# Projection and gate tiles: high and low activations as one 512-column matmul, second half of the bank added on VectorE

## What is computed

```python
def parallel_mixers(h, w_in, b_gate, ...):
    proj = h @ w_in          # 1024 -> qa ka va qb kb vb fb qc kc vc gates
    ...
    gates = jax.nn.sigmoid(gl.reshape(bsz, seq, N_BRANCHES, D_MODEL) + b_gate)
    merged = (gates[:, :, 0] * (ya @ w_out_a)
              + gates[:, :, 1] * (yb @ w_out_b)
              + gates[:, :, 2] * (yc @ w_out_c))
    return merged @ w_out
...
for l in range(DEPTH):
    ...
    h = rms_norm(x, norm1_g[l]) * (1.0 + sc1) + sh1
    x = x + g1 * parallel_mixers(h, ...)
    h = rms_norm(x, norm2_g[l]) * (1.0 + sc2) + sh2
    x = x + g2 * peer_ffn(h, ...)
```

## Time and profile before

| | |
|---|---|
| median of the runs | 2226.91 us |
| the profiled execution | 2227.43 us |
| its span, first to last instruction | 2225.6 us |
| TensorE (PE) busy | 97% of the span |
| VectorE (DVE) busy | 74% |
| ScalarE (ACT) busy | 55% |
| GpSimd (POOL) busy | 12% |
| mean granted TensorE clock | 0.989 of full speed |
| read from HBM | 425 MB, 191 GB/s |

### The profile page before, as it was taken

The page is one execution under the profiler, slowest core; times in us unless marked ns, Lnnn a source line. Parts: engine busy times, 40 slices in busy tenths (PEclk is TensorE's granted clock), DMA queues, the critical chain, the costliest instruction groups (busy, mean ns, idle before and its releaser), DMA issues.

```text
span 2225.6 us, 45150 instructions
## 1 busy us (share of the span) xinstructions
PE 2164.8 (97%) x14996; PEld 1996.6 (90%) x14996; DVE 1656.9 (74%) x3155; ACT 1217.0 (55%) x2134; POOL 268.7 (12%) x298
## 2 busy tenths in 40 slices
PE   4999999999999999999989999999999999999998
PEld 4889989999999988888878899899999999888887
DVE  6787766889589956777557868588895998567765
ACT  3656555444577654545455565644445776454544
POOL 0210000000157500000002100000001772000000
PEclk7999999999999999999999999999999999999999
DMA  8566655555533357787545666455555334588765
GB/s 321 169 209 216 209 171 169 180 180 178 185 127 114 114 195 255 253 257 229 196 174 171 224 213 214 138 182 183 180 184 174 114 113 135 195 274 256 254 214 162
DMA packets 114452, 427.48 MB, mean 192 GB/s; under 512 B 12704, under 2 KB 12960, under 8 KB 113056
## 3 DMA queue, kind: packets, MB, share of 16 engines
q1 hardware_dynamic: 114336, 426.08, 57.3%
HBM read 424.98 MB, written 1.05 MB: 191 GB/s over the span
## 4 chain that ended last, share of the span: by engine, by line
PE 94%; DVE 2%; issue 1%; DMA 1%; ACT 1%; POOL 0%; SPq 0%; ACTq 0%; DVEq 0%; POOLq 0%
PE pj L1290 18%; PE pj L1291 17%; PE pj L1292 17%; PE wk L1290 10%; PE wk L1292 10%; PE wk L1291 10%; PE wk L1602 5%; DMA arena<-in_front 1%; PE wk L1402 1%; PE wk L1379 1%; PE wk L1341 1%; PE wk L1395 1%; PE wk L1542 0%; PE wk L1315 0%; PE wk L1424 0%
## 5 line engine op out<-in xcount | busy, mean ns | idle before, releaser
L797 DVE TENSOR_TENSOR lo<-raw,hi 128x1024 fp32r<-128x1024 f32 x683 | 840.3, 1232 | 475.8 <-ACT hi L471 468.0
L471 ACT ACTIVATE hi<-raw 128x1024 fp32r<-128x1024 f32 x683 | 721.6, 1057 | 468.6 <-PE wk L1292 345.1
L1290 PE MATMUL pj<-mov_hi,hi 128*128 128x256 f32 x3248 | 945.5, 291 | 31.6 <-DVE mov_lo L848 27.5
L1291 PE MATMUL pj<-mov_lo,hi 128*128 128x256 f32 x3248 | 921.3, 284 | 0.0
L1292 PE MATMUL pj<-mov_hi,lo 128*128 128x256 f32 x3248 | 921.2, 284 | 0.0
L1290 PEld LDWEIGHTS pj<-mov_hi,hi 128*128 128x128 f32 x3248 | 624.2, 192 | 47.1 <-DVE mov_lo L848 30.4
L1291 PEld LDWEIGHTS pj<-mov_lo,hi 128*128 128x128 f32 x3248 | 625.9, 193 | 0.2
L1292 PEld LDWEIGHTS pj<-mov_hi,lo 128*128 128x128 f32 x3248 | 624.9, 192 | 0.0
L1290 PE MATMUL wk<-hi,mov_hi 128*128 128x512 f32 x1024 | 398.6, 389 | 1.7 <-DVE mov_lo L1239 1.7
L1292 PE MATMUL wk<-hi,mov_lo 128*128 128x512 f32 x1024 | 398.4, 389 | 0.0
L1291 PE MATMUL wk<-lo,mov_hi 128*128 128x512 f32 x1024 | 398.4, 389 | 0.0
(11 more groups left out here) (184 smaller groups left out, 1507.9 us busy)
## 6 DMA issues: line engine op xcount, KB each, us to landing
raw<-in_stream SPq DMA_DIRECT2D x684, 512.0 KB, 3.3
arena<-in_ada SPq DMA_DIRECT2D x72, 512.0 KB, 4.8
onehot_a<-in_ada SPq DMA_DIRECT2D x24, 512.0 KB, 4.6
arena<-in_front SPq DMA_DIRECT2D x4, 2048.0 KB, 19.3
arena<-in_taba SPq DMA_DIRECT2D x2, 1536.0 KB, 19.4
arena<-in_keys SPq DMA_DIRECT2D x2, 1024.0 KB, 6.3
x<-in_xT SPq DMA_DIRECT2D x1, 1024.0 KB, 5.0
arena<-in_mix SPq DMA_DIRECT2D x2, 512.0 KB, 16.1
```

What stands on the lines that cost most here:

```text
L471: nc.scalar.activation(hi[j % SPLIT][:, :], raw[j % RAW][:, :], ACT.Copy).then_inc(hi_done, 1)
L797: nc.vector.tensor_tensor(lo[j % SPLIT][:, :], raw[j % RAW][:, :], hi[j % SPLIT][:, :].bitcast(f32), ALU.subtract).then_inc(lo_done, 1)
L1290: pe.matmul(out, w_h, m_h, start=first, stop=False)
L1291: pe.matmul(out, w_h, m_l, start=False, stop=False)
```

## The change

The high and low activations of the 8 chunks are laid side by side in one buffer `mov`, so that 512 columns of one chunk are contiguous. For the 47 tiles of a layer that are neither V tiles nor outside the input projection, a new `project_half` issues two matmuls a chunk in place of three: the high weights by high and low activations at once, over all 512 columns of the bank, and the low weights by the high activations into the first 256. ScalarE evicts the first half as before, but raises a new semaphore `first_half`. VectorE then adds the second half to what was evicted (`second_half_of`), and it raises `out_free`. The new VectorE instruction for tile t-1 is put at the very start of VectorE's step t. All other stages keep three matmuls; they read `mov` through `mov_hi(k)`, `mov_lo(k)` and `mov_of`. The branch outputs and the one-hot buffers that used chunks 8 to 11 of the old buffers have their own `w_hi` and `w_lo`.

```diff
-        mov_hi = sb("mov_hi", [P, 12, SEQ], f32r)
-        mov_lo = sb("mov_lo", [P, 12, SEQ], f32r)
+        mov = sb("mov", [P, KC, 2, SEQ], f32r)
+        w_hi = sb("w_hi", [P, 4, SEQ], f32r)
+        w_lo = sb("w_lo", [P, 4, SEQ], f32r)
...
@@ evict, ScalarE @@
                     if t < N_QKV:
                         nc.scalar.activation(projT[:, t, :], pj[t % 2][:, 0:SEQ], ACT.Identity,
-                                             scale=HD ** -0.5 if QC <= t < QC + 4 else 1.0).then_inc(out_free, 1)
+                                             scale=HD ** -0.5 if QC <= t < QC + 4 else 1.0).then_inc(first_half, 1)
...
@@ VectorE @@
+                def second_half_of(t):
+
+                    if VB <= t < VB + 4 or VC <= t < VC + 4:
+                        return
+                    before = t - 4 * (t > VB) - 4 * (t > VC)
+                    dve.wait_ge(first_half, l * (DENSE - 8) + before + 1)
+                    if t in (VB + 4, VC + 4):
+
+                        dve.wait_ge(out_free, l * OUTS + t + 2)
+                    nc.vector.scalar_tensor_tensor(projT[:, t, :], pj[t % 2][:, SEQ:2 * SEQ],
+                                                   HD ** -0.5 if QC <= t < QC + 4 else 1.0, projT[:, t, :], ALU.mult,
+                                                   ALU.add).then_inc(out_free, 2 if t == DENSE - 1 else 1)
+
                 for t in range(DENSE):
+                    if t:
+                        second_half_of(t - 1)
...
                     if t in ADA_AT:
                         modulation(ADA_AT.index(t))
+                second_half_of(DENSE - 1)
                 rest_of(L0 + (DENSE + AHEAD), DENSE + AHEAD)
...
@@ TensorE @@
+                def project_half(t, j, o, bank, chunks=None, between=None):
+
+                    pe.wait_ge(lo_done, t + 1)
+                    pe.wait_ge(out_free, l * OUTS + o + 1)
+                    out = pj[bank][:, :]
+                    for k in range(KC):
+                        if chunks is not None:
+                            pe.wait_ge(mov_ready, l * M_READY + (chunks + k + 1))
+                        if between is not None and k == KC // 2:
+                            between()
+                        wh, wl = chunk(j, k)
+                        both = mov[:, k, :, :].rearrange("p a s -> p (a s)")
+                        if k < KC - 1:
+                            pe.matmul(out, wh, both, start=k == 0, stop=False)
+                            pe.matmul(out[:, 0:SEQ], wl, mov_hi(k), start=False, stop=False)
+                        else:
+                            pe.matmul(out[:, 0:SEQ], wl, mov_hi(k), start=False, stop=False)
+                            last = pe.matmul(out, wh, both, start=False, stop=True)
+                    return last
...
-                        project(L0 + t, t, t, t % 2, None if t else 0, between=lambda: late_pieces(t))\
+                        project_half(L0 + t, t, t, t % 2, None if t else 0, between=lambda: late_pieces(t))\
```

More of the change, by code:

```diff
@@ L220, in trunk, with mov_of, mov_hi, mov_lo @@
         F_BANK = (2, 4, 3, 5)
+        def mov_of(side, k, n):
+            return mov[:, k:k + n, side, :] if k < KC else (w_hi, w_lo)[side][:, k - KC:k - KC + n, :]
+        def mov_hi(k):
+            return mov_of(0, k, 1).squeeze(1)
+        def mov_lo(k):
+            return mov_of(1, k, 1).squeeze(1)
         def y_pairs(br, i):
@@ L1329, in project @@
                             between()
-                        last = product(pj[bank][:, 0:SEQ], *chunk(j, k), mov_hi[:, at[k], :], mov_lo[:, at[k], :],
+                        last = product(pj[bank][:, 0:SEQ], *chunk(j, k), mov_hi(at[k]), mov_lo(at[k]),
                                        k == 0, k == KC - 1)
+                    return last
[16 more added lines that the diff above has]
+                            last = pe.matmul(out, wh, both, start=False, stop=True)
                     return last
@@ L1614, in _ @@
                                 tokens(i, j, 1)
-                            last = product(pj[j % 2][:, 0:SEQ], *chunk(j, k), mov_hi[:, k, :], mov_lo[:, k, :],
+                            last = product(pj[j % 2][:, 0:SEQ], *chunk(j, k), mov_hi(k), mov_lo(k),
                                            k == 0, k == KC - 1)
```

32 lines of the change are left out of this document (15 added, 17 removed).

## The result

The changed kernel takes 2234.84 us (median of 6 runs, 2233.18 to 2241.35); the kernel before, in 6 runs beside it, 2226.72 us. The ratio is 1.0039, 95% interval [1.0028, 1.0050]: slower by 8.1 us, well clear of the interval, and just above the top of my range (2234.5). I had given "slower by over 0.2%" a chance of 0.32.

The account below looks back on a forecast made before the run. TensorE, busy 97% of the span, was taken as the bound. Savings of 7.2 us less 9.3 us of added waits gave net +2.1 us: 2229.0 us, no change that can be told; 8 in 10 range 2220.5 to 2234.5.

Parts of the forecast that it names:

- What TensorE saves: Projection and gate tiles: two matmuls a chunk save 0.107 us a tile; 67 tiles keep it, 7.2 us less.
- Step 34 (point 4): Addition behind the modulation of step 33, which waits for its transfer, delays stick pieces and TensorE's tails: +0.25 us a layer.
- The end of the gates (point 5): Tile 54 and first branch tile wait for additions behind modulations that wait for transfers: +3.64 and +3.02 us by layer.
- my own sign: End of the gates: reading falls if the first branch tile does not come some 3 us later against tile 50.
- I leave the landings where they are: End of the gates: the modulations' transfers were taken to land at unchanged times against the end of tile 50.
- The clock: Rival: TensorE's idle at the gates' end lowers the clock, up to 1.7 us each time; 2232 to 2236, chance 0.18.
- Tiles 9 to 12 and step 23 (points 2, 3): Additions ahead of the scores' reading delay the chain to GpSimd and TensorE: +0.68 and +0.40 us a layer.
- VectorE's additions: 94 new VectorE instructions, 0.48 us each, VectorE 37 to 45 us busier, hidden wherever VectorE has time.
- the gates with what follows: From tile 50 to first gelu: +6.7 us up to the first branch tile, 0 from there on.
- second-matmul rival: All changed tiles: a chunk saves 2.5 ns, not 13.4, by the skill's rule; result 2234.9, chance 0.07.

Follow-up runs that it names:

- experiment 3: Changed kernel with each tile's seven wide matmuls first, then eight narrow, then the last wide: 2241.15 us, ratio 1.0065 to the kernel before.
- experiment 7: As experiment 6, with the 256-column matmul ahead of the 512-column one in odd chunks: 2241.97 us, ratio 1.0059 to the kernel before.
- experiment 1: Changed kernel without VectorE's additions: two matmuls a chunk, ScalarE's eviction releases the bank; 2225.44 us, ratio 0.9991 to the kernel before.
- experiment 2: Kernel before's three matmuls a chunk, plus VectorE's 94 additions (times zero) and their semaphore chain: 2238.87 us, ratio 1.0047 to the kernel before.
- experiment 4: Changed kernel with 128 already met waits on TensorE ahead of the layers, shifting its instruction fetches: 2234.93 us, ratio 1.0032 to the kernel before.
- experiment 9: Changed kernel with VectorE's modulation of step 33 moved behind the stick pieces of step 34: 2233.95 us, ratio 1.0027 to the kernel before.
- experiment 6: Changed kernel with each modulation moved behind the addition of its step's tile in VectorE's program: 2243.68 us, ratio 1.0073 to the kernel before.
- experiment 5: Changed kernel with tiles 51 to 54 back to three matmuls and released by ScalarE: 2228.44 us, ratio 1.0000 to the kernel before.

## Why the prediction was wrong

**What TensorE saves: wrong, and the largest miss.** "Both widths carry the same 0.0134 us", so the eight removed matmuls save 0.107 us a tile. It saves 0.061 (2.881 less 2.82), and 0.09 in the orders of experiments 3 and 7. Two streams of one width were taken for the price of a mixture; I had the bound (nothing to 0.214) but took the value from the rows of unmixed streams. The measured 7.6 ns a chunk lie between the two prices I weighed, 2.5 of the rule and 13.4 of the rows. The term came to -3.5 us in place of -7.2: 67 tiles at 0.061 are -4.1, and some 0.5 us were lost between the places named (0.3 of it at tile 1 of layer two). The Trainium skill, "TensorE: Matmul & The Clock Gate", section "Back-to-back issue gap", has the 2.5 ns for the isolated gap, and says that in a stream with a weight load ahead of each matmul both set the distance. Such a load stands ahead of each matmul here; neither the distances of that 2.5 ns (0.325 us a chunk) nor one fixed part from the trace (0.347) fit the alternation, 0.353.

**Step 34 (point 4): right place, wrong size.** +2.6 us for +0.5. The step that failed is the 0.15 us by which the last stick piece ends ahead of TensorE's tails: I took it from the profile before, as if the landing kept its place against TensorE. In layer one TensorE came 0.2 us earlier by what it had saved, the transfer took 1.05 us longer to land, beside a fetch that the shorter program had moved there, and 0.25 is the addition: 1.5 us in sum, 1.48 measured (experiments 1, 2, 4 and 9).

**The end of the gates (point 5): the mechanism held, the size not.** +3.3 us for +6.7, and by my own sign (some 3 us later against tile 50; it was 1.9 and 1.4) the point fell. The sentence "I leave the landings where they are" failed in the other direction: in layer one the two transfers landed 0.6 and 1.1 us earlier, counted from tile 0, and TensorE came to tile 50 0.5 us later. Why they landed earlier is open, since without a fetch beside it step 52's transfer took 4.0 to 6.2 us in these runs. Experiment 2, where step 52's transfer took 4.9 and 5.2 us as in the kernel before, has 6.5 us of waits there.

**The clock: the rival came true on top of the forecast**, in layer one, for 1.5 us where I had given it up to 1.7. I had made it exclusive of a smaller stall; here it followed two waits of 0.8 and 1.75 us. The length of the waits does not decide it alone: it did not follow 1.34 and 2.34 us in layer one of experiment 2, nor 2.60 us in experiment 6, and did follow 2.49 us in experiment 7. The other 1.4 us up to the first gelu, in the second norms, I had at nothing, and nothing here ties them to the change.

**Tiles 9 to 12 and step 23 (points 2, 3): right**, +1.1 for +1.4 and +0.8 for +0.8; TensorE's waits for GpSimd at the transposes grew from 1.2 us to 2.7. The value tiles (+0.5) I had not seen.

**VectorE's additions: right in kind.** 0.421 us each and 32.8 us in sum for 37 to 45, and hidden in most places: without the four last tiles the kernel ties with the one before (experiment 5).

In sum: -3.5 for -7.2 is 3.7 us, step 34 2.1, the value tiles 0.5; less by 0.5 are the gates with what follows (6.2 for 6.7), and by 0.3 tiles 9 to 12 and step 23. The difference is 5.5 us, and 2.1 + 5.5 is the measured 7.6. That the gates with what follows came near my figure is chance: the waits were half of what I had, and the clock and the norms filled the gap. The time of the second-matmul rival (2234.9) is nearly the measured one for the same reason; its 2.5 ns are not what was measured.

## What to carry to other kernels

When work is moved onto an engine that runs in program order, look first at what in its program waits for a transfer: whatever is put behind that wait is as late as the transfer, however idle the engine is on average. A saving on the bounding engine lasts only until the next such meeting point, so find these first, and use the new form only where the time is kept (here 24 of 47 tiles, with three orders mended, beat all 47). Price a mixture of instructions from a mixture, not from two pure streams.

## What the runs showed of the hardware

- Matmuls of 512 and 256 columns in strict alternation take 0.236 + 0.117 us; in pairs of like width 0.233 + 0.115; pure streams 0.2268 and 0.1200.
- A 16 KB fetch of TensorE's program within half a microsecond of the issue of a 512 KB transfer went with a landing about 1 us later (5.1 us against 4.1), and moved with the fetch when 128 instructions were put in. The Trainium skill, "Runtime: NRT & Kernel Launch", section "Instruction fetch mechanics", calls the cost of crossing a 16 KiB boundary mostly hidden; for TensorE the trace agrees (its matmuls at 168.23, 168.35 and 168.58 us, around the packet, keep their distances), for the transfer beside it not.
- Without such a packet near, the same 512 KB transfer (step 52) landed after 4.0 to 6.2 us, from one kernel or layer to another.
- Two idle times of TensorE, 0.79 and 1.75 us with one tile between, were followed by 3.4 us at 0.50 of the clock in layer one, which cost 1.46 us; 0.9 and 1.1 us in layer two were not. One of 2.49 us was (experiment 7), one of 2.60 us was not (experiment 6).
